# A hybrid attention layer on one core: which of the first two weight units the program begins with

## The reference, cut to what matters

```python
h = rms_norm(x, norm_gain[l])                       # x: 256 x 2048, float32
proj = jnp.einsum('bsd,dn->bsn', h, w_in[l])        # 2048 x 13392 weights
(qa, ka, va, ga, qi, ki, wi, qb, kb, vb, gb, ma, mb) = jnp.split(proj, offsets, axis=-1)
...
ya = jnp.einsum('bsc,cd->bsd', oa * jax.nn.silu(ga), w_o_a[l])
yb = jnp.einsum('bsc,cd->bsd', ob * jax.nn.silu(gb), w_o_b[l])
merged = jax.nn.sigmoid(ma) * ya + jax.nn.sigmoid(mb) * yb
x = x + jnp.einsum('bsd,de->bse', merged, w_out[l])
```

## Time and profile before

| | us |
|---|---|
| median of three runs | 770.41 (770.40 to 770.61) |
| the profiled execution, its own time | 770.51 |
| its span, first to last instruction | 768.7 |
| PE busy | 764.8 (99%) |
| DVE busy | 516.9 (67%) |
| ACT busy | 431.1 (56%) |
| POOL busy | 135.8 (18%) |
| granted TensorE clock | 1.000 of full speed |

### The profile page before, as it was taken

One profiled execution on the slowest core, in us unless ns is written; L12 is line 12 of the kernel. 1 busy time (PEld: TensorE's weight loads), 2 busy tenths in 40 slices (PEclk: granted clock), 3 DMA queues, 4 the chain that ended last, 5 costly groups with the idle time before them and its releaser, 6 DMA issues.

```text
span 768.7 us, 10429 instructions
## 1 busy us (share of the span) xinstructions
PE 764.8 (99%) x3568; PEld 643.8 (84%) x3568; DVE 516.9 (67%) x724; ACT 431.1 (56%) x710; POOL 135.8 (18%) x225
## 2 busy tenths in 40 slices
PE   9999999999999999999999999999999999999998
PEld 8899988888888888888888888888888888888887
DVE  6768788888776755678656665767465567765553
ACT  6855756676663745555656565455576334444331
POOL 4412533322221000000212222312110011110000
PEclk9999999999999999999999999999999999999999
DMA  8988889998888675666866768767767888887553
GB/s 294 318 258 276 264 245 291 276 254 266 245 245 243 187 200 167 193 192 172 240 207 197 222 192 270 234 185 222 224 208 224 302 230 240 246 242 230 198 183 122
DMA packets 89612, 176.80 MB, mean 230 GB/s; under 512 B 7616, under 2 KB 15424, under 8 KB 89312
## 3 DMA queue, kind: packets, MB, share of 16 engines
q1 hardware_dynamic: 80752, 152.06, 65.8%
q0 software_dynamic: 8528, 23.87, 10.9%
q10 hardware_dynamic: 288, 0.30, 0.1%
HBM read 162.18 MB, written 14.02 MB: 229 GB/s over the span
## 4 chain that ended last, share of the span: by engine, by line
PE 99%; DMA 0%; DVE 0%; issue 0%
PE ps L760 29%; PE ps L762 29%; PE ps L761 29%; PE ps L774 1%; PE ps L778 1%; PE ps L794 1%; PE ps L795 1%; PE ps L784 1%; PE ps L860 0%; PE ps L963 0%; PE ps L962 0%; PE ps L961 0%; DMA xt<-in_x_columns 0%; PE ps L780 0%; PE ps L776 0%; PE ps L861 0%
## 5 line engine op out<-in xcount | busy, mean ns | idle before, releaser
L1332 DVE TENSOR_TENSOR lo<-raw,hi 128x1024 fp32r<-128x1024 f32 (+2 forms) x277 | 331.2, 1202 | 230.1 <-ACT hi L1041 229.3
L1041 ACT ACTIVATE hi<-raw 128x1024 fp32r<-128x1024 f32 (+2 forms) x277 | 286.3, 1038 | 291.5 <-PE ps L762 254.7
L760 PE MATMUL ps<-hi,hT_hi 128*128 128x512 f32 (+1 forms) x880 | 339.9, 386 | 0.0
L761 PE MATMUL ps<-lo,hT_hi 128*128 128x512 f32 (+1 forms) x880 | 339.0, 385 | 0.0
L762 PE MATMUL ps<-hi,hT_lo 128*128 128x512 f32 (+1 forms) x880 | 339.0, 385 | 0.0
L762 PEld LDWEIGHTS ps<-hi,hT_lo 128*128 128x128 f32 x880 | 165.2, 188 | 32.1
L760 PEld LDWEIGHTS ps<-hi,hT_hi 128*128 128x128 f32 x880 | 165.2, 188 | 31.5
L761 PEld LDWEIGHTS ps<-lo,hT_hi 128*128 128x128 f32 x880 | 165.2, 188 | 31.3
L760 PE MATMUL ps<-hi,ogT_hi 128*128 128x512 f32 x128 | 49.8, 389 | 0.0
L761 PE MATMUL ps<-lo,ogT_hi 128*128 128x512 f32 x128 | 49.8, 389 | 0.0
L762 PE MATMUL ps<-hi,ogT_lo 128*128 128x512 f32 x128 | 49.8, 389 | 0.0
(11 more groups left out here) (199 smaller groups left out, 665.1 us busy)
## 6 DMA issues: line engine op xcount, KB each, us to landing
raw<-in_w_in SPq DMA_DIRECT2D x190, 512.0 KB, 4.5
raw<-in_w_out SPq DMA_DIRECT2D x32, 512.0 KB, 4.2
raw<-in_w_o_a SPq DMA_DIRECT2D x16, 512.0 KB, 5.9
raw<-in_w_o_b SPq DMA_DIRECT2D x16, 512.0 KB, 4.2
raw<-in_w_in SPq DMA_DIRECT2D x16, 384.0 KB, 4.9
turned<-swapped POOLq DMA_DIRECT2D x12, 512.0 KB, 3.3
v<-turned POOLq DMA_DIRECT2D x32, 128.0 KB, 5.8
raw<-in_w_in SPq DMA_DIRECT2D x7, 336.0 KB, 4.6
```

What stands on the lines that cost most here:

```text
L760: mm(o, a_hi, w_hi[:, j], start=first and j == 0, stop=False)
L761: mm(o, a_hi, w_lo[:, j], start=False, stop=False)
L1041: activation(hi[:, slot, :, 0:width], raw[:, slot, :, 0:width], ACT.Copy).then_inc(hi_ready, 1)
L1332: tt(lo[:, slot, :, 0:width], raw[:, slot, :, 0:width], hi[:, slot, :, 0:width].bitcast(F32), ALU.subtract).then_inc(lo_ready, 1)
```

## The change

One line of the table changes. The program now begins with chunk 0's unit 0 (512 columns, packed); chunk 2's unit 0 (336 columns), which stood first, stands second.

```diff
-FIRST_UNITS = ((2, 0), (0, 0), (1, 0))
+FIRST_UNITS = ((0, 0), (2, 0), (1, 0))
 FIRST_UNITS += tuple(unit for i in range(1, CK) for unit in
                      ((0, i), (1, i)) + (((2, THIRD_BEHIND.index(i)),) if i in THIRD_BEHIND else ()))
```

## The result

| | before | after |
|---|---|---|
| median of 15 runs each, us | 770.50 (770.11 to 771.05) | 772.08 (770.79 to 772.89) |
| the profiled execution | 770.51 | 772.02 |
| its span | 768.7 | 770.2 |

The ratio is 1.0017, with a 95% interval of 1.001 to 1.0024. The changed kernel is slower by 1.3 us by that ratio and by 1.6 us by the medians, not by 0.4, and the median lies outside the stated range of 770.1 to 771.8. (Three of the fifteen runs of before are the ones shown ahead of the prediction.)

A forecast was written before the change was run, and what follows sets the result against it. PE, busy 99% of the span, bounds the kernel. The late load of u = 4 adds 0.40 us, hiding the first units' 0.2 us; from the median 770.41 this gives 770.8 us, range 770.1 to 771.8.

The forecast's parts named there:

- the pace of the first two units: PE's first two units at full pace, 1.26 and 0.92 us, so PE leaves them 0.2 us later.
- rival 3: TensorE's clock falls to 1.2 GHz in the longer pause before the first unit; +3.2 us beside 0.4, 774.0; chance 0.04.
- The bound, that 1.14 us of full-speed work decides: Under the slower clock, over 1.14 us of full-speed work run at 1.2 GHz makes the kernel slower by more than 0.2%.
- The start of PE: PE begins its first wide unit at 4.82 us, 0.44 us later than before.
- The rule of the Trainium skill: Software queue: about 2.0 us fixed plus bytes at 436 GB/s; 88 KB more costs 0.2 us, sum +0.33 us.
- upper bound: First 256 KB tile lands not before 3.68 us and not later than 4.04; the forecast took 4.04.
- The stalls in the first unit: Little is left of the first unit's 0.34 us of stalls; the wide unit takes 1.26 us.
- The load of u = 4: SP issues it at 7.77 us instead of 7.37, 0.40 us later, waiting for DVE's wide subtraction in round j = 1.
- I take it in full: The 0.40 us later issue of u = 4's load reaches PE whole; it lands at 12.90, PE begins at 14.02.
- rival 1: The later issue is hidden by queued bytes; u = 4 lands less than 0.2 us later, 770.3 to 770.6 us; chance 0.25.
- The +0.40 us: Whole shift, from the late u = 4 load; the first units' 0.2 us vanishes in that wait and isn't added.
- Rivals 2 and 4: Transfers in a worse pattern, 771.0 to 771.8 us, chance 0.12; first-unit stalls saved, shift -0.11 us, chance 0.01.

The follow-up runs named there:

- e2: Changed kernel with eight warm-up matmuls instead of seven; 770.88 us, 1 of 11 runs above 771.6.
- e11: Changed kernel, same seven warm-up matmuls begun later by a wait for POOL's second memset; 770.86 us.
- e7_before_eight_early: Kernel before with eight warm-up matmuls and round j = 1's first weight copy and subtraction moved ahead of the input tile's; 770.44 us.
- e4_before_eight: Kernel before with eight warm-up matmuls instead of seven; 770.55 us, 0 of 11 runs above 771.6.
- e1_before_six: Kernel before with six warm-up matmuls instead of seven; 771.93 us, 7 of 11 runs above 771.6.
- e5_before_late_first: Kernel before, PE's first unit held back until ACT has copied the first tile of two units; 772.28 us, 8 of 10 runs above 771.6.
- e10_after_again: Changed kernel timed once more without any edit; 772.22 us, 8 of 11 runs above 771.6.
- e12_before_late_nine: Kernel before with the first unit held back until two units' first tiles are copied, and nine warm-up matmuls instead of seven; 771.14 us.
- e9_before_six_shifted: Kernel before with six warm-up matmuls, begun later by a wait for POOL's second memset; 770.82 us, 1 of 11 runs above 771.6.
- e8_after_eight_early: Changed kernel with eight warm-up matmuls and round j = 1's first weight copy and subtraction moved ahead of the input tile's; 770.96 us.
- e3_after_seven_half: Changed kernel with one extra warm-up matmul of 64 columns after the seven; 772.45 us, 7 of 11 runs above 771.6.
- e6_after_ten: Changed kernel with ten warm-up matmuls instead of seven; 770.88 us, 0 of 11 runs above 771.6.

## Why the prediction was wrong

**The step that failed is the pace of the first two units.** The sum took them at full pace, 1.26 us and 0.92 us, and had PE leave them 0.2 us later. They took 2.30 us (4.73 to 7.03) and 1.68 us (7.03 to 8.71), and PE left them 1.91 us later, since TensorE was still at 1.2 GHz. The possibility was set aside as rival 3: the pause between warm-up and first unit grows (0.27 to 0.71 forecast, 0.63 in the profile), and the first units then run at 1.2 GHz. It got a chance of 0.04, and going by the run times it happened in 19 of 26 runs. Even there the mechanism was not quite the measured one: rival 3 has a clock that is up and falls in the pause, and the runs show one that has not yet risen. That is why the argument against it, a PEclk of 1.00 over the last 24 us with PE idle for 3.1, did not bear on it; and the same column could not have warned either, as it reads 1.00 at the start of the program where matmuls stand at half pace. In the trace of before the shortest warm-up record takes 421 ns, the lower level (e2's 274 is the other one), and the clock's record begins at 4.44 us, just as the first unit began. The prediction took the level as given, and should have asked since when it was up and what raised it.

**Rival 3's price** was set at 3.2 us beside 0.4, for three units at the lower level. In the profile two units ran there, which with the late start is 1.91 us, and 0.31 us came back at u = 4: 1.6 us there and 1.5 in the span. The bound, that 1.14 us of full-speed work decides, was too simple for the same reason.

**The start of PE was right in the profile, and partly by luck.** Forecast 4.82, measured 4.73. The first tile landed 3.29 us after its issue and its copy began at 4.04, so the row of its own size (3.3 us) decided. The rule of the Trainium skill for the software queue (DMA: Bandwidth & Descriptors, Anatomy of one DMA), by which 0.2 us instead of 0.4 were to be added, doesn't fit. But 4.04 was to be the upper bound, and it is the earliest of the seven profiles with the changed order; the other six lie between 4.13 and 4.37. **The stalls in the first unit were not gone.** In the changed kernel's profile none shows, but at half pace every operand is early. At full pace, in e2 and in e11, the first unit takes 1.60 and 1.59 us, not the forecast 1.26.

**The load of u = 4 was right in its issue and wrong in its effect.** The issue moved by 0.42 us (7.79), forecast 0.40. It waits for the low part of u = 0, as the prediction has it, and not of u - 3 = 1, as the section on the kernel says. But the transfer's landing hardly follows the issue. Here is what all the profiles show, issue and begin of ACT's copy, which waited for the transfer each time:

| kernel | issued | copied |
|---|---|---|
| e7_before_eight_early | 7.14 | 11.56 |
| before | 7.37 | 12.50 |
| e4_before_eight | 7.43 | 12.15 |
| e1_before_six | 7.53 | 11.99 |
| e5_before_late_first | 7.62 | 12.70 |
| after | 7.79 | 12.68 |
| e10_after_again | 7.89 | 12.60 |
| e12_before_late_nine | 7.95 | 11.67 |
| e9_before_six_shifted | 8.15 | 11.85 |
| e8_after_eight_early | 8.30 | 12.46 |
| e11_after_shifted | 8.46 | 12.09 |
| e3_after_seven_half | 8.49 | 12.37 |
| e2_after_eight | 8.55 | 12.23 |
| e6_after_ten | 8.62 | 12.60 |

From 7.37 to 8.62 us of issue the copy begins anywhere between 11.67 and 12.70, in no order. So the step "I take it in full" was wrong; the copy came 0.18 us later for an issue 0.42 us later, which is what rival 1 said.

**The +0.40 us of the lower group came out nearly right for another reason, which is luck.** With the level out of play the order costs 0.33 us (e2 against e4); the changed kernel's lower group lies at 770.87, 0.37 above the 770.50 of before. In e2's profile PE doesn't stand at u = 4 at all. There the sum reads: the first unit begins 0.49 us later (4.87), the first two units take 2.53 us instead of 2.42, +0.11, and the 0.31 us of standing at u = 4 are gone; together +0.29, and the second matmul of u = 4 is in fact 0.33 us later (14.29 against 13.96). So the forecast had the right size with the wrong terms: it dropped the late start as hidden by a wait, and in truth the late start stays and swallows the wait. That rests on profiles; e8, which was to test it, is weak.

**Rivals 2 and 4** did not happen: the later transfers kept their pattern, and PE did not begin nearly as early as before. And that PE's busy share bounds the kernel, so that an early shift reaches the end, held: 1.62 us at u = 4, 1.5 us in the span.

## What to carry to other kernels

A warm-up should last until the first real matmul. If it ends early by a few tenths of a microsecond more, hardly anything in the busy time, the waits or the chain shows it, but most runs can lose more than the change itself costs; here one more warm-up matmul, or the same seven begun 0.58 us later, took that away in ten of 11 runs each. Read TensorE's level from the spacing of equal matmuls, and look at single run times before the median: two groups with a gap were here a state that some runs had reached and others had not. A later issue of a load should not be priced in full without a second reading: here 0.42 us of issue moved the copy by 0.18.

## What the runs showed of the hardware that was not expected

- **The moment at which TensorE's level rises differs from run to run, and a pause in front of it can put it off by microseconds.** In the profiled executions it lies between 3.98 and 4.63 us (six kernels, e5 with PE idle at that moment among them), at 5.50, 6.18 and 6.19 (e6, e12, e4), or at 8.72 to 10.01 (after, e10, e8, e3 and e1, all with a pause of 0.53 us or more), and nowhere between 6.19 and 8.72. Kernels that are the same up to that moment differ: e4 and e7 have 6.19 and 4.11, e2 and e8 3.98 and 9.39. The Trainium skill (TensorE: Matmul & The Clock Gate, What's actually happening) states that the low level is the default, that activity releases it, and that the point varies by half a microsecond either way. The rows agree with the first two; the point varies more here, from 4.11 to 6.19 us even among the kernels with no pause over 0.32.
- **A pause with an effect that large is small in itself.** Going by the profiled pauses, 0.27 us before the first unit gave 1 run of 122 above 771.6 us; 0.63 to 1.03 us gave 34 of 47 (after, e10, e1 and e5). What exactly sets the edge stays open: e3, with half a matmul more than the changed kernel, had 7 of 11 and e2, with a whole one more, 1 of 11, though their profiled pauses are 0.56 and 0.55 us (e2's with a warm-up that the early rise had shortened by 0.19).
- **The lower level can be nearly free.** In e4 the first unit ran at half pace, which cost 0.54 us there and 0.26 at u = 4, as the rest went into a wait for a transfer that PE would have had anyway.
- **The same weight transfer can take 7.4 us in one run and 9.94 in another** (issued at 114.1 us, before and e9), and the stretch in which it came late put e9 2.0 us behind at the end.
